# Stick-breaking attention: triangle and ones products in two rounded passes, and the carry as a factor on the weighted values

## The reference, cut to what matters

```python
def stick_breaking_attention(q, k, v):
    """q,k,v: (B,S,H,Dh). A[t,s] = beta_ts * prod_{s<j<t}(1-beta_tj), s<t only."""
    ...
    def block(args):
        qi, bi = args
        z = jnp.einsum('bhqd,bhkd->bhqk', qi, kf).astype(jnp.float32) * scale
        qpos = bi * SB_BLOCK + jnp.arange(SB_BLOCK)
        before = kpos[None, :] < qpos[:, None]
        log_beta = jax.nn.log_sigmoid(z)
        log_1m = jnp.where(before, jax.nn.log_sigmoid(-z), 0.0)
        tail = lax.cumsum(log_1m, axis=3, reverse=True) - log_1m
        w = jnp.where(before, jnp.exp(log_beta + tail), 0.0)
        return jnp.einsum('bhqk,bhkd->bhqd', w.astype(vf.dtype), vf)
```

## Time and profile before

| | |
|---|---|
| median of 3 runs | 1162.07 us (1160.93 to 1162.46) |
| profiled execution, own time | 1161.97 us |
| its span, first to last instruction | 1160.2 us |
| busy: PE, PEld | 1082.9 us (93%), 845.5 us (73%) |
| busy: DVE, ACT, POOL | 808.4 us (70%), 573.5 us (49%), 76.1 us (7%) |
| mean granted TensorE clock | 0.968 of full speed |
| first triangle product of the stage | 280.05 us |
| last triangle product of the stage | 423.45 us |

### The profile page before, as it was taken

One profiled execution on the slowest core, in us unless ns is written; L12 is line 12 of the kernel. 1 busy time (PEld: TensorE's weight loads), 2 busy tenths in 40 slices (PEclk: granted clock), 3 DMA queues, 4 the chain that ended last, 5 costly groups with the idle time before them and its releaser, 6 DMA issues.

```text
span 1160.2 us, 12115 instructions
## 1 busy us (share of the span) xinstructions
PE 1082.9 (93%) x4844; PEld 845.5 (73%) x4844; DVE 808.4 (70%) x767; ACT 573.5 (49%) x705; POOL 76.1 (7%) x69
## 2 busy tenths in 40 slices
PE   6999999987899999838999999999999999999993
PEld 5877777876535458737888888878888878888782
DVE  2536657655454545777778777789876799867998
ACT  6313533357464640376665546653456543466353
POOL 0004113201101000400000000000000000000000
PEclk9999999978899999978999999999999999999997
DMA  7211112110000023060130310301303003016003
GB/s 220 78 45 37 37 37 73 36 38 1 1 1 1 20 102 114 37 236 1 37 109 1 109 37 21 125 1 37 109 1 114 31 19 127 1 43 248 1 1 145
DMA packets 44624, 70.44 MB, mean 61 GB/s; under 512 B 10228, under 2 KB 19736, under 8 KB 44568
## 3 DMA queue, kind: packets, MB, share of 16 engines
q1 hardware_dynamic: 43528, 69.66, 17.7%
q10 hardware_dynamic: 1040, 0.00, 0.1%
HBM read 61.27 MB, written 8.39 MB: 60 GB/s over the span
## 4 chain that ended last, share of the span: by engine, by line
PE 84%; DVE 8%; ACT 4%; issue 2%; DMA 1%; DVEq 0%; ACTq 0%
PE ps L648 25%; PE ps L652 25%; PE ps L650 25%; PE ps L864 2%; PE ps L724 1%; PE ps L877 1%; PE ps L787 1%; PE ps L892 1%; PE ps L832 1%; DVE sb_e L1663 1%; ACT sb_e L1233 1%; DVE out_gained L1888 1%; DMA g_pre_mix_c<-in_g_pre_mix 1%; ACT sb_w L1213 1%; DVE ps L1697 1%
## 5 line engine op out<-in xcount | busy, mean ns | idle before, releaser
L648 PE MATMUL ps<-a_op,b_op 128*128 128x512 f32 x448 | 175.9, 393 | 5.4 <-DVE b_op L1805 4.5
L648 PE MATMUL ps<-b_op,a_op 128*128 128x512 f32 x448 | 174.6, 390 | 2.7 <-issue 2.7
L650 PE MATMUL ps<-a_op,b_op 128*128 128x512 f32 x448 | 175.6, 392 | 0.0
L652 PE MATMUL ps<-a_op,b_op 128*128 128x512 f32 x448 | 175.4, 392 | 0.0
L652 PE MATMUL ps<-b_op,a_op 128*128 128x512 f32 x448 | 174.3, 389 | 0.0
L650 PE MATMUL ps<-b_op,a_op 128*128 128x512 f32 x448 | 174.3, 389 | 0.0
L648 PE MATMUL ps<-act_hi,w_hi 128*128 128x512 f32 x288 | 115.0, 399 | 3.2 <-DVE w_lo L1455 3.2
L1805 DVE TENSOR_TENSOR b_op<-wq,b_op 128x1024 fp32r<-128x1024 f32 x96 | 116.9, 1218 | 0.0
L1347 ACT CAST a_op<-f 128x1024 fp32r<-128x1024 f32 x56 | 58.8, 1049 | 116.0 <-PE ps L652 75.7
L652 PE MATMUL ps<-act_hi,w_lo 128*128 128x512 f32 x288 | 112.8, 392 | 0.0
L650 PE MATMUL ps<-act_lo,w_hi 128*128 128x512 f32 x288 | 112.6, 391 | 0.0
(11 more groups left out here) (190 smaller groups left out, 1759.5 us busy)
## 6 DMA issues: line engine op xcount, KB each, us to landing
wq<-in_w_ff_in SPq DMA_DIRECT2D x16, 1024.0 KB, 5.3
wq<-in_w_ff_out SPq DMA_DIRECT2D x16, 1024.0 KB, 5.1
stage<-in_w_in SPq DMA_DIRECT2D x18, 512.0 KB, 4.7
y<-in_x SPq DMA_DIRECT2D x4, 1024.0 KB, 10.0
stage<-in_w_out SPq DMA_DIRECT2D x8, 512.0 KB, 3.7
h_spill<-y SPq DMA_DIRECT2D x8, 512.0 KB, 3.0
h_back<-h_spill SPq DMA_DIRECT2D x1, 4096.0 KB, 15.5
out<-y SPq DMA_DIRECT2D x8, 512.0 KB, 2.7
```

The costliest lines, as they stand in the source:

```text
L648: nc.tensor.matmul(dst, stat[0], mov[0], start=first, stop=False, skip_group_check=chained)
L650: nc.tensor.matmul(dst, stat[0], mov[1], start=False, stop=False, skip_group_check=chained)
L652: return nc.tensor.matmul(dst, stat[1], mov[0], start=False, stop=last, skip_group_check=chained)
```

## The change

The triangle product and the ones product take the logs in two rounded passes. ACT rounds `sb_l` to `sb_hi` (type fp32r), DVE puts the rest, `sb_l` minus `sb_hi`, into `sb_lo`, and TensorE multiplies each part by the table, itself rounded at the start of the stage by two ACT casts. `sb_hi` lies on the buffer of `sb_e`, `sb_lo` on that of `sb_l`.

The carry no longer goes onto the scores. The ones table becomes two tables of 128 x 128, one per head, each with -1 in 64 columns, so that both heads add into bank 6, on the 64 partitions each where their values product lands. ACT takes exp of these sums (`sb_rest`). The values product of a step is no longer summed over the chain in PSUM: each step writes bank 4 or 7 by itself, and DVE (`add_output`) multiplies it by `sb_rest` and adds it to the output tile in SBUF, two steps behind; where the step is wider than the one before, the new queries are copied instead. At the end of the stage DVE does this for the last two steps, and the bank copy of ACT is gone.

```diff
--- before.py
+++ after.py
-        sb_carry = at("sb_carry", [P, 2, BANK], X_AT + 32 * K)
-        neg_tri = at("neg_tri", [P, P], X_AT + 36 * K)
-        neg_ones = at("neg_ones", [P, P], X_AT + 36 * K + 512)
+        sb_hi = at("sb_hi", [P, 2, 2, BANK], ACT_AT + 16 * K, F32R)
+        sb_lo = at("sb_lo", [P, 2, 2, BANK], ACT_AT + 24 * K, F32R)
+        sb_rest = at("sb_rest", [P, 2, BANK], X_AT + 32 * K)
+        tri_r = at("tri_r", [P, P], X_AT + 36 * K, F32R)
+        ones_r = at("ones_r", [P, 2, P], X_AT + 36 * K + 512, F32R)
+        neg_ones = at("neg_ones", [P, P], X_AT + 38 * K)
+        neg_tri = at("neg_tri", [P, P], X_AT + 38 * K + 512)
+        pair_ones = at("pair_ones", [P, 2, P], X_AT + 39 * K)
+        sb_part = at("sb_part", [P, BANK], X_AT + 38 * K)
...
             pool.wait_ge(v_turned, 2)
+            nc.gpsimd.memset(pair_ones[:, :, :], 0.0)
             after(nc.gpsimd.memset(neg_ones[:, :], -1.0))
+            for a in range(2):
+                nc.gpsimd.memset(pair_ones[:, a, HEAD * a:HEAD * (a + 1)], -1.0)
...
-                masked(pe, s, log_raw, log_masked)
-                if adds(s):
-                    pe.wait_ge(carry_added, adds(s))
+                pe.wait_ge(l_lo_ready, s + 1)
                 for a in range(2):
-                    mm = nc.tensor.matmul(ps[:, 2 * (s % 2) + a, c0:], neg_tri[:, :],
-                                          sb_l[:, s % 2, a, c0:], start=False, stop=True,
-                                          skip_group_check=True)
+                    bank = ps[:, 2 * (s % 2) + a, c0:]
+                    nc.tensor.matmul(bank, tri_r[:, :], sb_hi[:, s % 2, a, c0:], start=False,
+                                     stop=False, skip_group_check=True)
+                    mm = nc.tensor.matmul(bank, tri_r[:, :], sb_lo[:, s % 2, a, c0:],
+                                          start=False, stop=True, skip_group_check=True)
                 mm.then_inc(expo_ready, 1)
             def carry(s):
                 c0 = SB[s][3]
                 if adds(s):
-                    pe.wait_ge(carry_copied, adds(s))
+                    pe.wait_ge(rest_ready, adds(s))
                 elif s == 0:
                     pe.wait_ge(win_copied, 2)
                 for a in range(2):
-                    mm = nc.tensor.matmul(ps[:, 6 + a, c0:], neg_ones[:, :],
-                                          sb_l[:, s % 2, a, c0:], start=first_of_chain(s),
-                                          stop=True, skip_group_check=True)
+                    nc.tensor.matmul(ps[:, 6, c0:], ones_r[:, a, :], sb_hi[:, s % 2, a, c0:],
+                                     start=first_of_chain(s) and a == 0, stop=False,
+                                     skip_group_check=True)
+                    mm = nc.tensor.matmul(ps[:, 6, c0:], ones_r[:, a, :], sb_lo[:, s % 2, a, c0:],
+                                          start=False, stop=a == 1, skip_group_check=True)
                 mm.then_inc(carry_ready, 1)
             def weighted(s):
                 p, half, j, c0 = SB[s]
                 masked(pe, s, w_raw, w_masked)
-                if first_of_chain(s):
-                    if chain_of(s):
-                        pe.wait_ge(o_copied, chain_of(s))
-                    else:
-                        pe.wait_ge(win_pt, 4)
+                if s >= 2:
+                    pe.wait_ge(o_added, s - 1)
+                elif s == 0:
+                    pe.wait_ge(win_pt, 4)
+                else:
+                    pe.wait_ge(win_copied, 2)
                 for a in range(2):
                     mm = nc.tensor.matmul(
-                        ps[HEAD * a:HEAD * (a + 1), 4, c0:],
+                        ps[HEAD * a:HEAD * (a + 1), 4 + 3 * (s % 2), c0:],
                         vtok[:, j, P * p + HEAD * a:P * p + HEAD * (a + 1)],
-                        sb_w[:, s % 2, a, c0:], start=first_of_chain(s),
-                        stop=last_of_chain(s), skip_group_check=True)
+                        sb_w[:, s % 2, a, c0:], start=True, stop=True, skip_group_check=True)
                 mm.then_inc(pv_done, 1)
...
-            pe.wait_ge(tables_ready, 2)
+            pe.wait_ge(tables_rounded, 2)
...
-            def output_copy(s):
-                p, half = SB[s][:2]
-                act.wait_ge(pv_done, s + 1)
-                nc.scalar.copy(o_t[p][:, BANK * half:BANK * (half + 1)], ps[:, 4, :])\
-                    .then_inc(o_copied, 1)
+            act.wait_ge(tables_ready, 2)
+            nc.scalar.copy(tri_r[:, :], neg_tri[:, :]).then_inc(tables_rounded, 1)
+            nc.scalar.copy(ones_r[:, :, :], pair_ones[:, :, :]).then_inc(tables_rounded, 1)
...
                 if s:
                     weights_exp(s - 1)
+                masked(act, s, log_raw, log_masked)
+                nc.scalar.copy(sb_hi[:, s % 2, :, c0:], sb_l[:, s % 2, :, c0:])\
+                    .then_inc(l_hi_ready, 1)
                 if not first_of_chain(s):
                     c1 = SB[s - 1][3]
                     act.wait_ge(carry_ready, carries(s - 1))
-                    if adds(s) > 1:
-                        act.wait_ge(carry_added, adds(s) - 1)
-                    nc.scalar.copy(sb_carry[:, :, c1:], ps[:, 6:8, c1:]).then_inc(carry_copied, 1)
-                if s >= 2 and last_of_chain(s - 2):
-                    output_copy(s - 2)
+                    if s >= 2:
+                        act.wait_ge(o_added, s - 1)
+                    nc.scalar.activation(sb_rest[:, s % 2, c1:], ps[:, 6, c1:], ACT.Exp)\
+                        .then_inc(rest_ready, 1)
...
+            def rest_log(s):
+                c0 = SB[s][3]
+                dve.wait_ge(l_hi_ready, s + 1)
+                nc.vector.tensor_tensor(sb_lo[:, s % 2, :, c0:], sb_l[:, s % 2, :, c0:],
+                                        sb_hi[:, s % 2, :, c0:].bitcast(F32), ALU.subtract)\
+                    .then_inc(l_lo_ready, 1)
+            n_parts = [0]
+            def add_output(s):
+                p, half, j, c0 = SB[s]
+                part = ps[:, 4 + 3 * (s % 2), :]
+                total = o_t[p][:, BANK * half:BANK * (half + 1)]
+                dve.wait_ge(pv_done, s + 1)
+                if first_of_chain(s):
+                    nc.vector.tensor_copy(total[:, c0:], part[:, c0:]).then_inc(o_added, 1)
+                    return
+                c1 = SB[s - 1][3]
+                if c0 < c1:
+                    nc.vector.tensor_copy(total[:, c0:c1], part[:, c0:c1])
+                dve.wait_ge(rest_ready, adds(s))
+                dve.wait_ge(o_added, s)
+                nc.vector.tensor_tensor(sb_part[:, c1:], part[:, c1:], sb_rest[:, s % 2, c1:],
+                                        ALU.mult).then_inc(part_ready, 1)
+                n_parts[0] += 1
+                dve.wait_ge(part_ready, n_parts[0])
+                nc.vector.tensor_tensor(total[:, c1:], total[:, c1:], sb_part[:, c1:], ALU.add)\
+                    .then_inc(o_added, 1)
...
-                if not first_of_chain(s):
-                    c1 = SB[s - 1][3]
-                    dve.wait_ge(log_raw, s + 1)
-                    dve.wait_ge(carry_copied, adds(s))
-                    z = ps[:, 2 * (s % 2):2 * (s % 2) + 2, c1:]
-                    nc.vector.tensor_tensor(z, z, sb_carry[:, :, c1:], ALU.add)\
-                        .then_inc(carry_added, 1)
+                if s >= 2:
+                    add_output(s - 2)
                 for n in range(early(s - 1) if s else 0, early(s)):
                     recurrent_row(n)
                 if s + 1 < len(SB):
                     minus_abs(s + 1)
+                rest_log(s)
...
+            for s in range(len(SB) - 2, len(SB)):
+                add_output(s)
```

More of the change, by code:

```diff
@@ L227, in encoder_layer @@
             sem("z_ready"), sem("z_abs"), sem("sp_ln"), sem("log_raw"), sem("log_masked"))
-        carry_ready, carry_copied, carry_added = (
-            sem("carry_ready"), sem("carry_copied"), sem("carry_added"))
-        expo_ready, w_raw, w_masked, pv_done, o_copied = (
+        l_hi_ready, l_lo_ready, tables_rounded = (
+            sem("l_hi_ready"), sem("l_lo_ready"), sem("tables_rounded"))
+        carry_ready, rest_ready, part_ready = (
+            sem("carry_ready"), sem("rest_ready"), sem("part_ready"))
+        expo_ready, w_raw, w_masked, pv_done, o_added = (
             sem("expo_ready"), sem("w_raw"), sem("w_masked"),
-            sem("pv_done"), sem("o_copied"))
+            sem("pv_done"), sem("o_added"))
         sq_summed = sem("sq_summed")
@@ L518, in block_of @@
                 return w[rows:rows + BANK, cols:cols + BANK].rearrange("(k p) n -> p k n", p=P)
-            sp.wait_ge(carry_added, adds(len(SB) - 1))
+            sp.wait_ge(o_added, len(SB))
             sp.dma_start(wq11[:, :, :], block_of(0, 0, 0)).then_inc(wq_loaded[0], 16)
@@ L913, in recurrent_out @@
                         pe.wait_ge(y_added, N_EARLY)
-                        pe.wait_ge(carry_copied, adds(len(SB) - 1))
```

(8 more changed lines are left out.)

## The result

The changed kernel takes 1184.1 us (median of 4 runs, 1181.9 to 1184.5), the one before 1162.1 us on the same chip: a ratio of 1.019, 95% interval 1.018 to 1.020. The forecast was 1176 us with a range of 1166 to 1187.

What follows compares the result with a forecast made beforehand. The stage was taken as PE-bound with DVE close behind. Span 1160.2 + 9.2 at full clock + 5 for the clock = 1174.4, with 1.8 around it 1176 us; range 1166 to 1187.

Steps and rivals of the forecast that it cites:

- rival A: Full steps: the clock falls in nearly every second one, 9.2 + 16 us more, 1187 us; chance 17%.
- Steps at the full clock: Steps s = 7 to 23: wide steps gain, narrow ones lose, 102.9 us against 102.7 before, +0.2 us.
- Start: Stage start up to s = 3: ACT's cast and what queues behind it wait for the log, +5.2 us.
- 3 to 7: Steps s = 3 to 7: 23.8 us at full clock, against 21.7 for the same widths later, +2.2.
- the ring: Stage steps: scores, DVE's sign and subtraction, then triangle product in a closed loop; a full pair 15.59 us against 15.46.
- 7 to 11: Four full steps, the first with a short multiply: 29.2 us against 30.3 before.
- End: From the last triangle product until PE may go on to bank 6: 5.6 us against 4.0, +1.6.
- the one for the clock: Twenty steps after the start: low clock about three times more, 1.6 us each, +5 us, bounds 0 and +16.
- the sum at the full clock: Whole stage without clock changes: 5.2 + 2.2 + 0.2 + 1.6 = +9.2 us.
- B: Rival on PE's clock in the stage: it costs nothing more, 1171 us; chance 13%.
- D: Rival, no change: the ring holds, but ring and start are shorter than counted and the clock holds, 1162 us; chance 6%.
- C: Rival, faster: DVE's sign and subtraction hidden ahead of the triangle product, PE's 24 us back whole, 1138 us; chance 4%.

Runs made afterwards that it cites:

- e11: The changed kernel without VectorE's subtraction, both rounded passes reading sb_hi, so the low part of the logs is left out: 1159.3 us.
- e5: The changed kernel with 30 extra rounded 512-column products, unused, in steps 1 to 6 while PE would wait for sb_lo: 1175.8 us.
- e1: The changed kernel with VectorE's subtraction for step s ahead of the sign operation for step s+1 instead of behind it: 1178.2 us.

## Why the prediction was right, and where it was off

The direction and the mechanism held: PE waits for DVE's subtraction before nearly every triangle product (26.1 us, before 3.8), and what it sheds is eaten by this wait and by the low clock. Without the subtraction 24.8 us come back (e11 against after), to about the time of the kernel before. The size held only roughly: the change cost 22.0 us where 14 were forecast, and the measured time lies nearer to the 1187 us of rival A than to the 1176 of the forecast. It is in the range because the range was drawn out to A.

- **Steps at the full clock: held.** 11 to 15 took 22.44 us (forecast 22.3), 15 to 19 23.33 (23.2), the step s = 8 8.23 (8.11), s = 7 with its short multiply 7.01 (7.48 less some 0.5). The waits were 1.57 and 1.30 us (1.7), those for bank 5 0.79 to 1.38 (1.1). PE's busy share from 320 to 420 is 78% (75 to 80).
- **Start: +7.6 us at s = 3** (301.96 against 294.33), forecast +5.2. 1.0 of it stems from ahead of the stage; the sum was made at the full clock, and nearly all of it ran at the low one.
- **3 to 7: 31.44 us, forecast 23.8.** This is the step that failed, and it is the clock, not the ring: the first 16.6 us, up to 318.6, ran at 0.50. The two numbers should not be compared as they stand, though. The sum booked +2.2 over the 21.7 us that these widths take at the full clock, but the kernel before took 320.75 - 294.33 = 26.4 us here, with low clock of its own. What the sum stands for is 26.4 + 2.2 = 28.6 us, and the miss is 2.8.
- **7 to 11: 31.16 (29.2), 19 to 23: 31.72 (28.2).** One and two stays of 3.4 us at the low level, 349 to 353, 417 to 421 and 427 to 431.
- **End: 5.95 (5.6)**, and 1.5 behind it, with a stay from 448 on.

So the mis-sized term is the one for the clock. The measured 22.0 us less the 9.2 of the sum at the full clock leave 12.8 us, where I had put 5 with bounds of 0 and 16. They divide by the blocks above into 1.0 from ahead of the stage, 4.2 in the start and in 3 to 7, 6.9 with the stays behind the start and 0.6 in the rest. I had assumed some three more stays of 1.6 us in the twenty steps after the start, "beyond what the start had and keeps". Behind the start there were four (349, 417, 427, 448), of 1.7 us each: near that. But the start did not keep what it had: its three stays of 3.4 us between 280 and 305 became one of 37.5 us. That is the 4.2 us for which the prediction had nothing; putting work into the start, as e5 does, gives back 5.5 to 8.3 us. I had not asked of the start what I asked of every full step: how much rest PE gets there in the changed kernel.

Rival A (1187 us) had the size nearly right with the wrong place: in the full steps the clock fell three times, not in nearly every second one. B and D fall by the 54.3 us of low clock; C falls by e11, where even without the subtraction PE's 24 us do not come back, because ACT's exponential is late next. The sum named DVE alone as what could stop C.

## What to carry to other kernels

When a change takes work off the engine that is last and puts a short operation on another in front of it, follow the queue of that other engine: here 24 us less on PE bought 22 us more in all. Price the wait twice, in itself and by what PE's clock does with it, and do so first for stretches where PE rests already. And if there is independent work, put it in the gap between the producer and the consumer before judging the change: the same instructions in another order were worth 17 us to the changed kernel. Then give the kernel before the same layout: here it gained 10 us by it, and the change is to be judged against that one. Judged so, it was still 8.7 us slower.

## What the runs showed that I had not expected

- The clock can stay low while PE does not rest. From 302 to 309 us PE was busy all of the 7.00 us, with narrow and one-column products among them, and the clock stayed at 0.50; in the kernel before it came back within the same window. What made the difference is not settled.

```profile
302.00:309.00 7.00, 7.00 (x26) 4.96 (x26) 0.00 (x0) 1.02 (x1) 0.00 (x0) 0.50 0.01 2
```

- Products whose result nobody uses made a kernel faster: 30 of them, 8.3 us (e5).
- At the low clock a rounded pass of 128 columns costs as much as one of 256: 312.38 - 312.17 = 0.21 us, and two of 256 columns took 288.66 - 288.23 = 0.43. One of 512 took 0.43 by itself. At the full clock the narrow one was cheaper (e1: two of 128 columns in 361.94 - 361.77 = 0.17 us, two of 256 in 367.18 - 366.94 = 0.24).
